# Moving rows of a float32r matmul stored back to front and read with a step of -1

## The reference

```python
def swiglu_ffn(x, w_gu, w_down):                 # FFN_HIDDEN = 2816, two layers
    g, u = jnp.split(x @ w_gu, 2, axis=-1)
    return (jax.nn.silu(g) * u) @ w_down

def hybrid_layer(...):                           # two layers, D_FF = 4096
    z = rmsnorm(x, norm_mix) @ w_in
    ...
    x = x + mixed @ w_out
    u = jax.nn.relu(rmsnorm(x, norm_ffn) @ w_ff1)
    return x + (u * u) @ w_ff2
```

## Time and profile before

| | |
|---|---|
| median of 3 runs | 1346.08 us (1345.7 to 1346.67) |
| the profiled execution's own time | 1345.26 us |
| its span in the trace | 1343.5 us |
| TensorE busy with matmuls | 1314.9 us, 98% |
| VectorE, ScalarE, GpSimd busy | 944.1, 676.0, 58.9 us |
| DMA | 227.80 MB, 168 GB/s from HBM |

### The profile page before, as it was taken

The page is one execution under the profiler, slowest core; times in us unless marked ns, Lnnn a source line. Parts: engine busy times, 40 slices in busy tenths (PEclk is TensorE's granted clock), DMA queues, the critical chain, the costliest instruction groups (busy, mean ns, idle before and its releaser), DMA issues.

```text
span 1343.5 us, 25805 instructions
## 1 busy us (share of the span) xinstructions
PE 1314.9 (98%) x10699; PEld 1246.5 (93%) x10699; DVE 944.1 (70%) x1277; ACT 676.0 (50%) x838; POOL 58.9 (4%) x31
## 2 busy tenths in 40 slices
PE   5899999999999999999999999999999999999999
PEld 4699999988999999998989999998898999999988
DVE  8966976657865986657897787775457867877542
ACT  5774643334765643344666545444445554544332
POOL 6910000000000000000000000000000000000000
PEclk9999999999999999999999999999999999999999
DMA  8676586675443576666444446567664535556661
GB/s 157 159 187 185 133 218 186 188 189 182 145 145 97 155 210 185 188 190 175 149 141 143 155 160 217 189 182 194 188 188 126 157 122 194 189 187 187 188 188 63
DMA packets 342808, 227.80 MB, mean 170 GB/s; under 512 B 22616, under 2 KB 337792, under 8 KB 342592
## 3 DMA queue, kind: packets, MB, share of 16 engines
q1 hardware_dynamic: 341200, 226.33, 58.6%
q10 hardware_dynamic: 1520, 0.20, 0.1%
HBM read 224.40 MB, written 1.05 MB: 168 GB/s over the span
## 4 chain that ended last, share of the span: by engine, by line
PE 86%; DVE 7%; ACT 4%; issue 1%; POOL 1%; DMA 0%; SPq 0%; DVEq 0%; ACTq 0%; POOLq 0%
PE PS L419 20%; PE PS L420 20%; PE PS L421 20%; PE PS L429 12%; PE PS L430 6%; DVE w_lo L400 2%; ACT w_hi L395 1%; PE PS L1340 1%; DVE xn L1134 1%; DVE xn L1129 1%; DMA c_rows<-in_ssm_c_re_dram 0%; PE PS L1742 0%; PE PS L2409 0%; PE PS L1324 0%; DVE raw_lo L1089 0%
## 5 line engine op out<-in xcount | busy, mean ns | idle before, releaser
L400 DVE TENSOR_TENSOR w_lo<-raw,w_hi 128x2048 fp32r<-128x2048 f32 x207 | 473.5, 2290 | 144.1 <-ACT w_hi L395 143.0
L419 PE MATMUL PS<-x_hi,w_hi 128*128 128x256 f32 x1792 | 504.0, 281 | 0.9 <-DVE w_lo L400 0.5
L420 PE MATMUL PS<-x_lo,w_hi 128*128 128x256 f32 x1792 | 503.7, 281 | 0.0
L421 PE MATMUL PS<-x_hi,w_lo 128*128 128x256 f32 x1792 | 503.3, 281 | 0.0
L395 ACT ACTIVATE w_hi<-raw 128x2048 fp32r<-128x2048 f32 x207 | 396.4, 1915 | 203.3 <-PE PS L430 139.1
L419 PEld LDWEIGHTS PS<-x_hi,w_hi 128*128 128x128 f32 x1792 | 338.3, 189 | 6.0 <-issue 2.9
L420 PEld LDWEIGHTS PS<-x_lo,w_hi 128*128 128x128 f32 x1792 | 336.6, 188 | 0.1
L421 PEld LDWEIGHTS PS<-x_hi,w_lo 128*128 128x128 f32 x1792 | 336.7, 188 | 0.0
L429 PE MATMUL PS<-hid_both,w_hi 128*128 128x512 f32 x756 | 264.8, 394 | 0.0
L430 PE MATMUL PS<-hid_both,w_lo 128*128 128x256 f32 x756 | 211.8, 280 | 0.0
L429 PEld LDWEIGHTS PS<-hid_both,w_hi 128*128 128x128 f32 x756 | 142.1, 188 | 31.4
(11 more groups left out here) (394 smaller groups left out, 1481.5 us busy)
## 6 DMA issues: line engine op xcount, KB each, us to landing
raw<-in_w_ff_dram SPq DMA_DIRECT2D x128, 512.0 KB, 4.6
raw<-in_ffn_w_gu_dram SPq DMA_DIRECT2D x88, 512.0 KB, 5.1
raw<-in_w_in_dram SPq DMA_DIRECT2D x68, 512.0 KB, 4.7
raw<-in_sb_w_qkv_dram SPq DMA_DIRECT2D x24, 512.0 KB, 4.5
raw<-in_ffn_w_down_dram SPq DMA_DIRECT2D x20, 512.0 KB, 4.9
raw<-in_ssm_w_glu_dram SPq DMA_DIRECT2D x16, 512.0 KB, 5.5
raw<-in_w_out_dram SPq DMA_DIRECT2D x16, 512.0 KB, 4.5
raw<-in_ssm_w_out_dram SPq DMA_DIRECT2D x8, 512.0 KB, 4.6
```

The lines of the kernel that those rows point to most:

```text
L400: nc.vector.tensor_tensor(w_lo[s][:, :], raw[s][:, :], w_hi[s][:, :].bitcast(F32), ALU.subtract).then_inc(lo_done, 1)
L419: nc.tensor.matmul(dst, lhs_hi, r_hi, start=start, stop=False, skip_group_check=True)
L420: nc.tensor.matmul(dst, lhs_hi, r_lo, start=False, stop=False, skip_group_check=True)
L421: return nc.tensor.matmul(dst, lhs_lo, r_hi, start=False, stop=stop, skip_group_check=True)
```

## The change

Of inputs 0, 1, 3, 5 and 7 the rows of `x_hi` and `x_lo` are stored with token 255 in the first word and token 0 in the last, and every view of them has a step of -1, so that a matmul still takes token 0 first. Inputs 2, 4 and 6 stay as they were. All rows of `hid_both` are turned in the same way, the high and the low part together: in memory the low part comes first and the view is one run of 512 words with a step of -1. In the two FFN paths VectorE reads its source backwards and writes the row forwards; elsewhere ScalarE and VectorE write through the view with the step of -1. The matmuls' shapes, the weight loads, the DMAs and the order on each engine are the same.

```diff
-        x_hi = sb("x_hi", [P, KT, T], "xh", 0, F32R)
-        x_lo = sb("x_lo", [P, KT, T], "xl", 0, F32R)
-        hid_both = sb("hid_both", [P, 32, 2, T], "hh", 0, F32R)
+        def backwards(rows, but=()):
+            return [rows if i in but else rows[:, :, ::-1] for i in range(8)]
+        BY_TOKEN = {g.x for g in gemms if g.tokens}
+        x_hi = backwards(sb("x_hi", [P, KT, T], "xh", 0, F32R), BY_TOKEN)
+        x_lo = backwards(sb("x_lo", [P, KT, T], "xl", 0, F32R), BY_TOKEN)
+        hid_rows = sb("hid_rows", [P, 32, 2, T], "hh", 0, F32R)
+        hid_both = hid_rows[:, :, ::-1, ::-1]
         hid_hi, hid_lo = hid_both[:, :, 0, :], hid_both[:, :, 1, :]
...
-                        a, b = x_hi[:, kt, :], x_lo[:, kt, :]
+                        a, b = x_hi[g.x][:, kt, :], x_lo[g.x][:, kt, :]
...
-                    hi = hid_hi[:, bass.ds(idx, 1), :].rearrange("p a t -> p (a t)")
-                    lo = hid_lo[:, bass.ds(idx, 1), :].rearrange("p a t -> p (a t)")
+                    lo, hi = (hid_rows[:, bass.ds(idx, 1), i, :].rearrange("p a t -> p (a t)") for i in range(2))
+                    turned = prod[:, T - 1::-1]
...
-                    nc.vector.tensor_copy(hi, prod[:, 0:T]).then_inc(gated_hi, 1)
+                    nc.vector.tensor_copy(hi, turned).then_inc(gated_hi, 1)
                     dve.wait_ge(gated_hi, n)
-                    nc.vector.tensor_tensor(lo, prod[:, 0:T], hi.bitcast(F32), ALU.subtract).then_inc(hid_done, 1)
+                    nc.vector.tensor_tensor(lo, turned, hi.bitcast(F32), ALU.subtract).then_inc(hid_done, 1)
...
-                nc.vector.tensor_tensor(x_lo[:, 2 * q:2 * q + 2, :], res[:, 2 * q:2 * q + 2, :],
-                                        x_hi[:, 2 * q:2 * q + 2, :].bitcast(F32), ALU.subtract).then_inc(xl_done, 2)
+                nc.vector.tensor_tensor(x_lo[x_index(n)][:, 2 * q:2 * q + 2, :], res[:, 2 * q:2 * q + 2, :],
+                                        x_hi[x_index(n)][:, 2 * q:2 * q + 2, :].bitcast(F32), ALU.subtract).then_inc(xl_done, 2)
```

More of the change, by code:

```diff
@@ L470, in glu_first @@
                         dst = PS[:, bank_of(g, 0), m * T:(m + 1) * T]
-                        nc.tensor.matmul(dst, hi[:, kt, m, :], x_hi[:, kt, :], start=kt + m == 0, stop=False, skip_group_check=True)
-                        nc.tensor.matmul(dst, lo[:, kt, m, :], x_hi[:, kt, :], start=False, stop=False, skip_group_check=True)
+                        nc.tensor.matmul(dst, hi[:, kt, m, :], x_hi[0][:, kt, :], start=kt + m == 0, stop=False, skip_group_check=True)
+                        nc.tensor.matmul(dst, lo[:, kt, m, :], x_hi[0][:, kt, :], start=False, stop=False, skip_group_check=True)
                     if kt == 0:
@@ L476, in glu_first @@
                     for m in range(2):
-                        last = nc.tensor.matmul(PS[:, bank_of(g, 0), m * T:(m + 1) * T], hi[:, kt, m, :], x_lo[:, kt, :], start=False,
+                        last = nc.tensor.matmul(PS[:, bank_of(g, 0), m * T:(m + 1) * T], hi[:, kt, m, :], x_lo[0][:, kt, :], start=False,
                                                 stop=kt == KT - 1, skip_group_check=True)
@@ L487, in glu_second @@
                     for kt in range(KT):
-                        nc.tensor.matmul(dst, hi[:, kt, m, :], x_hi[:, kt, :], start=kt + m == 0, stop=False, skip_group_check=True)
-                        nc.tensor.matmul(dst, hi[:, kt, m, :], x_lo[:, kt, :], start=False, stop=False, skip_group_check=True)
+                        nc.tensor.matmul(dst, hi[:, kt, m, :], x_hi[0][:, kt, :], start=kt + m == 0, stop=False, skip_group_check=True)
+                        nc.tensor.matmul(dst, hi[:, kt, m, :], x_lo[0][:, kt, :], start=False, stop=False, skip_group_check=True)
                 weights_split(pe, 1)
@@ L493, in glu_second @@
                     for kt in range(KT):
-                        last = nc.tensor.matmul(dst, lo[:, kt, m, :], x_hi[:, kt, :], start=False, stop=kt == KT - 1,
+                        last = nc.tensor.matmul(dst, lo[:, kt, m, :], x_hi[0][:, kt, :], start=False, stop=kt == KT - 1,
                                                 skip_group_check=True)
@@ L669, in body @@
                     dve.wait_ge(hid_done, idx + g.hid0)
-                    hi = hid_hi[:, bass.ds(idx * 2, 2), :]
-                    lo = hid_lo[:, bass.ds(idx * 2, 2), :]
+                    lo, hi = (hid_rows[:, bass.ds(idx * 2, 2), i, :] for i in range(2))
+                    turned = gate_sb[:, k, :].rearrange("p (a t) -> p a t", a=2)[:, :, ::-1]
                     nc.vector.scalar_tensor_tensor(out=gate_sb[:, k, :].rearrange("p (a t) -> p a t", a=2),
@@ L1118, in gained_lo @@
             dve.wait_ge(xh_done, KT * x_index(n) + t + 1)
-            nc.vector.scalar_tensor_tensor(out=x_lo[:, t, :], in0=res[:, t, :], scalar=gain(n, t), in1=x_hi[:, t, :].bitcast(F32),
+            nc.vector.scalar_tensor_tensor(out=x_lo[x_index(n)][:, t, :], in0=res[:, t, :], scalar=gain(n, t),
+                                           in1=x_hi[x_index(n)][:, t, :].bitcast(F32),
                                            op0=ALU.mult, op1=ALU.subtract).then_inc(xl_done, 1)
@@ L1139, in high @@
                     for t in (2 * q, 2 * q + 1):
-                        nc.vector.tensor_scalar(x_hi[:, t, :], res[:, t, :], gain(4, t), None, ALU.mult).then_inc(xh_done, 1)
+                        nc.vector.tensor_scalar(x_hi[4][:, t, :], res[:, t, :], gain(4, t), None, ALU.mult).then_inc(xh_done, 1)
                     return
-                nc.vector.tensor_copy(x_hi[:, 2 * q:2 * q + 2, :], res[:, 2 * q:2 * q + 2, :]).then_inc(xh_done, 2)
+                nc.vector.tensor_copy(x_hi[x_index(n)][:, 2 * q:2 * q + 2, :], res[:, 2 * q:2 * q + 2, :]).then_inc(xh_done, 2)
             def low(q):
@@ L2262, in s5_vector @@
                 dve.wait_ge(xh_done, f + 1)
-                V.tensor_tensor(x_lo[:, f, :], gelu[:, f, :], x_hi[:, f, :].bitcast(F32), ALU.subtract).then_inc(xl_done, 1)
+                V.tensor_tensor(x_lo[0][:, f, :], gelu[:, f, :], x_hi[0][:, f, :].bitcast(F32), ALU.subtract).then_inc(xl_done, 1)
             dve.wait_ge(lo_done, 1)
```

12 lines of the change are left out of this document (6 added, 6 removed).

## The result

The changed kernel takes 1354.71 us (median of 4, 1354.25 to 1355.93) against 1345.92 us, a ratio of 1.0065 with a 95% interval of 1.0053 to 1.0078: 8.8 us slower. It is the side of the rival "slower, by worse meetings", at a third of that rival's price, and inside the stated range's slower part; the forecast of 1320 us was on the wrong side.

The account below looks back on a forecast made before the run. TensorE was taken to bound the kernel, by how fast one matmul follows another. 1345.3 us (profiled) - 26.6 on touched matmuls + 0.5 at product heads = 1319.2; the median is 0.8 higher, so 1320 us, range 1293 to 1372.

Parts of the forecast that it names:

- slower, by worse meetings: At every touched matmul, turned rows and weights stay together longer once they meet: 23.9 us more, 1370 us; chance 0.20.
- What bounds the kernel: Whole kernel: TensorE is busy for 98% of the span at full clock, so how fast one matmul follows another counts.
- The excess belongs to the meeting of two streams: On TensorE, 11.2 ns excess per single matmul and 29.1 per pair, read as collisions of moving rows with next weights.
- What a touched matmul will take: 5316 singles and 756 pairs: 114 ns a single instead of 117.9, 7.8 ns less a pair, 26.6 us saved.
- The distance changes by 3 words now and by 1 after: fewer meetings: On TensorE, per weight word, with both streams running down, the distance between them changes less: fewer meetings, if longer ones.
- no difference: The excess belongs to the moving stream alone, the same in both directions: time stays at 1346 us; chance 0.14.
- VectorE and ScalarE: Backward accesses may lose the casts' double rate; mostly covered, at five product heads 0 to 2.7 us, taken as 0.5.
- Half rate: At touched matmuls, backward rows are read at one word a cycle, not two: 2086 us; chance 0.08.
- The stretches that stay forward: Inputs 4 and 6 and early chunks keep their steps; if they moved too, the cause would not be direction.

Follow-up runs that it names:

- bursts: Three kernels without the computation, only bursts of the kernel's matmuls at varied weight offsets (high/low, in words), directions and entries; three matmuls settled between 346.7 and 360.0 ns.
- x only: Against the kernel before, only the normalised inputs' rows are turned, the hidden rows stay forward: 1345.77 us, ratio 1.0001 (0.9991 to 1.0011).

## Why the prediction was wrong

*What bounds the kernel.* Right: of the 9.0 us, 7.9 are longer steps from start to start, at the granted clock of before.

*The excess belongs to the meeting of two streams.* Right in that it depends on both: bursts that change nothing but the weights' offsets and the entry move three matmuls between 346.7 and 360.0 ns, and rows' direction and first word move it too. That the streams collide is not shown. The rule quoted from the Trainium skill ("TensorE: Matmul & The Clock Gate", section "Step-by-step: what each phase is for"), that loading the next weights takes nothing from the running matmul, would leave the time alone when only the weights move. This case's runs do not agree: moving the weights alone from 12/10 to 0/4 took 0.35% off the kernel. What the weight load takes from the matmul, or the matmul from the weight load, no run tells.

*"What a touched matmul will take."* This is the step that failed. It took the fastest single steps of an early chunk, 0.11 us, as what most matmuls would reach once the streams ran the same way. But single steps within a group are not independent: in `gu1` of the kernel before 116, 117 and 120 ns come again and again, one pattern whose sum, 353.3, is what stays. A short step is paid for by its neighbours, so the minimum of a chunk is no step that a stage can have. Turned rows settle at 117.8 or 120.0 ns, never at 114; a pair at 353.3, not 341. So in place of -20.7 us singles gave +4.3 us (2.8 from x, 1.5 from the hidden rows), and pairs +3.6 in place of -5.9. The stretch that was to show it, `ff1` of layer 0, did not move at all: 118.0 ns before and after, with every row of it turned.

*"The distance changes by 3 words now and by 1 after: fewer meetings."* Fallen as an argument for a gain. No setting of backward rows settled under 353.3 ns for three matmuls or for a pair, while forward rows reach 346.7 in both. No run turned the weight loads, so whether the two directions count together or the rows' alone stays open.

*The rival "slower, by worse meetings".* The right sign. Of its two reasons, "read downwards, the row begins at its high end" has some support, since one word on takes three backward matmuls from mostly 353.3 to 360.0 ns; "streams that go the same way stay together longer" was not tested. The price, +3.5 ns everywhere, was too high: the pairs paid 2.4 ns a matmul on average (1.9 to 3.3 by stage), the singles some 2 ns in some stretches and nothing in others. What it missed is that one stretch can have several steps.

*The rival "no difference".* It has what half of the touched singles did: `gu1`, both `ff1` and the mix of layer 1, 2784 of the 5316, kept their step. The pairs, `gu0`, the mix of layer 0 and the GLU did not, and 0.65% is clear of no difference.

*VectorE and ScalarE.* The 0.5 us at the heads was not there, and the double rate of the casts survives a backward source: 428 and 295 ns against 427 and 294.

*Half rate.* Excluded. The rule of the Trainium skill ("SBUF — State Buffer", section "SBUF: two separate sides") that accesses within a 16-byte line go at full bandwidth agrees with the trace here: a step of -1 costs 0 to 3.3 ns on a matmul, not 97.

*The stretches that stay forward.* They keep their steps only nearly: in x only, forward pairs went from 174.4 to 173.3 ns. The test that the prediction proposed there would have misled, since what runs ahead can change the step of unchanged code.

Open: the rule by which a lock is chosen, and the cause of 3.3 ns as the distance between most of them. Executions of one of these kernels differ by 1 to 4 us. Stretches that lock now one way, now the other, could explain it, but so could the preparation, whose end alone differs by 2.7 us between traces; only one execution of each kernel was traced.

## What to carry to other kernels

When TensorE alternates a weight load and a float32r matmul without a gap, as here, a few per cent of its step can hang on where moving rows and weights stand in SBUF and in which direction the rows are read (346.7 to 360.0 ns for three matmuls; 1341.6 to 1359.1 us for the whole kernel); it is settled by measuring, not by an argument on collisions. Measure such a step as the sum over a whole repeating group and over a whole stage, from several moments of entry, since one setting can have steady steps 2 to 4% apart (353.3 and 360.0 ns backward at 12/10, 346.7 and 360.0 forward at 0/0). An edit ahead of a stage can change the step of that stage without touching it, so two halves of a change need not add up, and an effect below 0.5% in such a kernel should be read stage by stage before it is credited to the edit.

## What was not expected of the hardware

Same code, same addresses, same clock, two steady rates: 353.3 and 360.0 ns for three backward matmuls, behind a first matmul of 132 or 134 columns, in two programs alike; and both in one stage of the changed kernel, ahead of and behind a pause. Most settled sums over a group lie on a ladder of 3.3 ns: 346.7, 350.0, 353.3, 356.7, 360.0, that is 8 periods of the 2.4 GHz clock between rungs; some lie between, as the forward pair's 348.9. In the bursts, with 0 to 2 GB/s of DMA in the stretches read and VectorE at rest, the steps were those of the full kernel, so neither of them is needed for it. The fastest pair seen took 340.0 ns (forward rows at 0/14, one burst of four, the others between 351.1 and 356.7), 20 ns over the 320 that 768 columns take at 2.4 GHz.
